# A hybrid attention block on one core: the start of the first projection in halves and product by product, without blank matmuls

## What is computed

```python
u = rms_norm(h, norm_gain)                    # h is x, 512 x 2048
proj = einsum('bsd,de->bse', u, w_in)         # 2048 x 13392
(q_sb, k_sb, v_sb, z_sb, q_sa, k_sa, v_sa, z_sa, q_ix, k_ix, w_ix, g_sb, g_sa) = split(proj)
y_sb = (stick_breaking(q_sb, k_sb, v_sb) * silu(z_sb)) @ w_branch_sb
y_sa = (sparse(q_sa, k_sa, v_sa, q_ix, k_ix, w_ix) * silu(z_sa)) @ w_branch_sa
h = h + (sigmoid(g_sb) * y_sb + sigmoid(g_sa) * y_sa) @ w_out
out = rms_norm(h, final_norm_gain)
```

## Time and profile before

| what | value |
|---|---|
| median of three runs | 1597.24 us (1597.21 to 1597.38) |
| the profiled execution, its own time | 1597.08 us |
| its span, first to last instruction | 1595.5 us |
| PE busy | 1585.0 us, 99% |
| DVE busy | 821.9 us, 52% |
| ACT busy | 572.5 us, 36% |
| DMA read from HBM | 156.9 MB |

### The profile page before, as it was taken

How to read it: one execution, slowest core, us unless ns; L and a number is a source line. 1 busy time by engine, 2 the same in 40 slices (tenths; PEclk the granted TensorE clock), 3 DMA queues, 4 the chain that set the end, 5 groups by cost and what they waited for, 6 DMA issues and landing times.

```text
span 1595.5 us, 19959 instructions
## 1 busy us (share of the span) xinstructions
PE 1585.0 (99%) x7138; PEld 1317.2 (83%) x7138; DVE 821.9 (52%) x1183; ACT 572.5 (36%) x851; POOL 15.8 (1%) x35
## 2 busy tenths in 40 slices
PE   9999999999999999999999999999999999999997
PEld 7788888888888888888888888888888888888886
DVE  6853678522126655556564546554545545434333
ACT  5542333222224444334453332343332533323232
POOL 0000000000000000000000000000000000000000
PEclk9999999999999999999999999999999999999999
DMA  7223323333333333333334334333433522253223
GB/s 225 82 79 93 93 80 93 106 92 85 100 105 96 111 108 110 111 106 104 106 117 132 109 102 113 98 116 110 115 91 122 181 101 92 96 204 121 98 100 118
DMA packets 97979, 176.39 MB, mean 111 GB/s; under 512 B 11264, under 2 KB 24080, under 8 KB 97296
## 3 DMA queue, kind: packets, MB, share of 16 engines
q1 hardware_dynamic: 93712, 160.60, 33.4%
q0 software_dynamic: 3040, 13.63, 2.3%
q10 hardware_dynamic: 1184, 1.58, 0.3%
HBM read 156.90 MB, written 8.39 MB: 104 GB/s over the span
## 4 chain that ended last, share of the span: by engine, by line
PE 97%; ACT 1%; DVE 1%; DMA 1%; issue 0%; SPq 0%; ACTq 0%; DVEq 0%
PE proj L1178 29%; PE proj L1179 29%; PE proj L1180 29%; PE attn L1179 3%; PE attn L1180 3%; PE attn L1178 3%; DMA xs<-in_x 1%; PE attn L1313 1%; PE attn L1312 1%; ACT junk L463 0%; ACT w_hi L410 0%; DVE w_lo L721 0%; DVE xs L764 0%; DVE area L764 0%; ACT u_hi L443 0%
## 5 line engine op out<-in xcount | busy, mean ns | idle before, releaser
L1178 PE MATMUL proj<-u_hi,w_hi 128*128 128x512 f32 x1536 | 600.5, 391 | 0.5 <-DVE u_lo L774 0.5
L1180 PE MATMUL proj<-u_hi,w_lo 128*128 128x512 f32 x1536 | 598.9, 390 | 0.0
L1179 PE MATMUL proj<-u_lo,w_hi 128*128 128x512 f32 x1536 | 598.8, 390 | 0.0
L721 DVE TENSOR_TENSOR w_lo<-stage,w_hi 128x1024 fp32r<-128x1024 f32 x266 | 323.5, 1222 | 458.7 <-ACT w_hi L410 457.2
L410 ACT ACTIVATE w_hi<-stage 128x1024 fp32r<-128x1024 f32 x266 | 280.1, 1056 | 430.9 <-PE proj L1180 302.2
L1178 PEld LDWEIGHTS proj<-u_hi,w_hi 128*128 128x128 f32 x1536 | 288.8, 188 | 60.2 <-issue 1.3
L1180 PEld LDWEIGHTS proj<-u_hi,w_lo 128*128 128x128 f32 x1536 | 288.5, 188 | 60.2
L1179 PEld LDWEIGHTS proj<-u_lo,w_hi 128*128 128x128 f32 x1536 | 288.8, 188 | 58.7
L1178 PE MATMUL proj<-w_hi,u_hi 128*128 128x512 f32 x256 | 99.9, 390 | 0.0
L1180 PE MATMUL proj<-w_hi,u_lo 128*128 128x512 f32 x256 | 99.8, 390 | 0.0
L1179 PE MATMUL proj<-w_lo,u_hi 128*128 128x512 f32 x256 | 99.8, 390 | 0.0
(11 more groups left out here) (175 smaller groups left out, 1413.0 us busy)
## 6 DMA issues: line engine op xcount, KB each, us to landing
stage<-in_w_in SPq DMA_DIRECT2D x208, 512.0 KB, 3.7
stage<-in_w_out SPq DMA_DIRECT2D x32, 512.0 KB, 3.6
x_in<-turned SPq DMA_DIRECT2D x256, 40.0 KB, 1.9
stage<-in_w_branch_sb SPq DMA_DIRECT2D x16, 512.0 KB, 3.6
stage<-in_w_branch_sa SPq DMA_DIRECT2D x16, 512.0 KB, 4.1
xs<-in_x SPq DMA_DIRECT2D x8, 512.0 KB, 8.0
o_scratch<-og POOLq DMA_DIRECT2D x16, 256.0 KB, 2.3
hres<-in_x POOLq DMA_DIRECT2D x1, 4096.0 KB, 13.6
```

The source lines that it names most:

```text
L721: V.tensor_tensor(w_lo[:, s % RING, :, :], stage[:, s % 2, :, :], w_hi[:, s % RING, :, :].bitcast(F), ALU.subtract).then_inc(strip_lo, 1)
L1178: nc.tensor.matmul(out_, a_hi, b_hi, start=start, stop=False, skip_group_check=free)
L1179: nc.tensor.matmul(out_, a_hi, b_lo, start=False, stop=False, skip_group_check=free)
L1180: return nc.tensor.matmul(out_, a_lo, b_hi, start=False, stop=stop, skip_group_check=free)
```

## The change

- SP loads the first slab of x and the first strip of W in halves of 128 channels or rows (256 KB each), in turns: x half 0, W half 0, x half 1, W half 1. The x halves have rows of 512 bytes. Each first half has a semaphore of its own (x_first, first_loaded).
- Strip 2 of W is put ahead of slab 3 of x (it was behind slab 4), and strip 3 ahead of slab 5 (it was behind slab 7).
- DVE, no longer ACT, makes the upper part of the first W half (`tensor_copy`, L789 of the new file), and makes its lower part before u_lo(0); the second W half's lower part comes before u_lo(1).
- PE issues no blank matmuls. The first strip is issued product by product: four matmuls hi times hi, then hi times lo, then lo times hi, each group with its own wait. turn_x(1) stands behind the first group.

```diff
--- before.py
+++ after.py
@@ -121,7 +121,6 @@
     ixw_lo = at("ixw_lo", [KT, KW], R, work + 6 * TILE + 8 * KT * KW)
     junk = at("junk", [D_MODEL], F, place["u_lo"] + 12 * TILE)
     gain_rows = at("gain_rows", [P], F, place["late"])
-    blank = at("blank", [CW], R, place["late"] + 4 * P)
     rstd_row = at("rstd_row", [SEQ], F, place["late"] + 4 * P + 4 * CW)
     rstd_cols = at("rstd_cols", [QT, P], F, work + 14 * TILE)
 
@@ -217,10 +216,11 @@
     gain_loaded, ixw_loaded, consts, masks = sem("gain_loaded"), sem("ixw_loaded"), sem("consts"), sem("masks")
     sumsq, norm_step, rooted = sem("sumsq"), sem("norm_step"), sem("rooted")
     cols_ready, cols_turned, row_ready = sem("cols_ready"), sem("cols_turned"), sem("row_ready")
+    x_first, first_loaded = sem("x_first"), sem("first_loaded")
     first_hi, first_lo = sem("first_hi"), sem("first_lo")
     raw_ready, raw_scaled, un_hi_ready, un_lo_ready = (
         sem("raw_ready"), sem("raw_scaled"), sem("un_hi_ready"), sem("un_lo_ready"))
-    gain_turned, gain_ready, blank_ready = sem("gain_turned"), sem("gain_ready"), sem("blank_ready")
+    gain_turned, gain_ready = sem("gain_turned"), sem("gain_ready")
     xt_done, u_hi_ready, u_lo_ready = sem("xt_done"), sem("u_hi_ready"), sem("u_lo_ready")
     ixw_hi_ready, ixw_lo_ready, kw_done, kw_scaled = sem("ixw_hi_ready"), sem("ixw_lo_ready"), sem("kw_done"), sem("kw_scaled")
     kix_hi_ready, kix_lo_ready = sem("kix_hi_ready"), sem("kix_lo_ready")
@@ -307,16 +307,18 @@
             def first_strip(s):
                 load_strip(C_QIX, s, rows(win)(s)[:, :, COL_QIX:COL_QIX + CW])
 
-            load_x(0)
-            first_strip(0)
+            for k, x_sem, w_sem in ((0, x_first, first_loaded), (1, x_loaded[0], strip_loaded[0])):
+                sp.dma_start(xs[:, :, P * k:P * k + P], x_cols[:, :, P * k:P * k + P]).then_inc(x_sem, 16)
+                sp.dma_start(stage[:, 0, k, :], rows(win)(0)[:, k, COL_QIX:COL_QIX + CW]).then_inc(w_sem, 16)
             load_x(1)
             first_strip(1)
-            for p in range(2, 5):
-                load_x(p)
+            load_x(2)
             first_strip(2)
+            load_x(3)
+            load_x(4)
+            first_strip(3)
             for p in range(5, NS):
                 load_x(p)
-            first_strip(3)
             sp.dma_start(ixw[:, :, :], win[:, :, COL_KIX:COL_KIX + KW]).then_inc(ixw_loaded, 16)
             for s in range(4, NS):
                 first_strip(s)
@@ -470,9 +472,8 @@
             act.wait_ge(gain_ready, 1)
             turned_high(0)
             act.wait_ge(strip_loaded[0], 16)
-            A(w_hi[:, 0, 0, :], stage[:, 0, 0, :], ACT.Copy).then_inc(first_hi, 1)
+            A(w_hi[:, 0, 1, :], stage[:, 0, 1, :], ACT.Copy).then_inc(strip_hi, 1)
             turned_high(1)
-            A(w_hi[:, 0, 1, :], stage[:, 0, 1, :], ACT.Copy).then_inc(strip_hi, 1)
             split_hi(0, 1)
             turned_high(2)
             turned_high(3)
@@ -750,7 +751,6 @@
                 step(V.tensor_tensor(rstd[:, cols], y_, t_, ALU.mult))
 
 
-            V.memset(blank[:, :].bitcast(F), 0.0).then_inc(blank_ready, 1)
             for h in range(HEADS):
                 V.memset(slope[:, h:h + 1], -(2.0 ** (-8.0 * (h + 1) / HEADS)))
             dve.wait_ge(masks, 2)
@@ -785,15 +785,17 @@
                     V.tensor_tensor(by_tile(u_lo[:, k, :]), raw_u(k), by_tile(u_hi[:, k, :].bitcast(F)),
                                     ALU.subtract).then_inc(un_lo_ready, 1)
 
-            dve.wait_ge(gain_ready, 1)
-            turned_low(0)
+            dve.wait_ge(first_loaded, 16)
+            V.tensor_copy(w_hi[:, 0, 0, :], stage[:, 0, 0, :]).then_inc(first_hi, 1)
             dve.wait_ge(first_hi, 1)
             V.tensor_tensor(w_lo[:, 0, 0, :], stage[:, 0, 0, :], w_hi[:, 0, 0, :].bitcast(F),
                             ALU.subtract).then_inc(first_lo, 1)
-            turned_low(1)
+            dve.wait_ge(gain_ready, 1)
+            turned_low(0)
             dve.wait_ge(strip_hi, 1)
             V.tensor_tensor(w_lo[:, 0, 1, :], stage[:, 0, 1, :], w_hi[:, 0, 1, :].bitcast(F),
                             ALU.subtract).then_inc(strip_lo, 1)
+            turned_low(1)
             turned_raw(0)
             turned_raw(1)
             split_lo(0, 1)
@@ -1219,7 +1221,9 @@
                         steps[s]()
 
             def turn_x(k):
-                if k % 2 == 0:
+                if k == 0:
+                    pe.wait_ge(x_first, 16)
+                elif k == 1 or k % 2 == 0:
                     pe.wait_ge(x_loaded[k // 2], 16)
                 if k >= HEAD_START:
                     pe.wait_ge(raw_ready, bank_user(k) + 1)
@@ -1234,35 +1238,32 @@
                 if ts[-1] == KT - 1:
                     m.then_inc(kw_done, 1)
 
-            def keep_busy(n):
-
-                for _ in range(n):
-                    nc.tensor.matmul(proj[3][:, :], blank[:, 0:P], blank[:, :], start=True, stop=True)
-
-            pe.wait_ge(blank_ready, 1)
-            keep_busy(4)
             pe.wait_ge(masks, 1)
             pe.wait_ge(gain_loaded, 16)
             nc.tensor.transpose(kw_bank[:, 0:KT], gain_rows[0:KT, :], ident[0:KT, 0:KT]).then_inc(gain_turned, 1)
-            keep_busy(1)
             turn_x(0)
-            turn_x(1)
-            keep_busy(4)
 
             def first_strip():
 
                 for j in range(2):
-                    pe.wait_ge(u_lo_ready, j + 1)
-                    if j == 0:
-                        pe.wait_ge(first_lo, 1)
-                    else:
+                    def products(w, u, first=False):
+                        for e in range(4):
+                            m = nc.tensor.matmul(proj[e][:, :], w[:, 0, j, P * e:P * e + P], u[:, j, :],
+                                                 start=first, stop=False)
+                        return m
+
+                    if j:
                         turn_x(2)
                         turn_x(3)
-                        pe.wait_ge(strip_lo, 1)
-                    for e in range(4):
-                        cols = slice(P * e, P * e + P)
-                        m = mm3(proj[e][:, :], w_hi[:, 0, j, cols], w_lo[:, 0, j, cols],
-                                u_hi[:, j, :], u_lo[:, j, :], j == 0, False)
+                    pe.wait_ge(u_hi_ready, j + 1)
+                    pe.wait_ge(strip_hi if j else first_hi, 1)
+                    products(w_hi, u_hi, first=j == 0)
+                    if j == 0:
+                        turn_x(1)
+                    pe.wait_ge(u_lo_ready, j + 1)
+                    products(w_hi, u_lo)
+                    pe.wait_ge(strip_lo if j else first_lo, 1)
+                    m = products(w_lo, u_hi)
                 m.then_inc(strip_used, 1)
 
             def between_strips(s):
```

## The result

| | before | with the change |
|---|---|---|
| median of 20 runs each | 1597.52 us (1596.98 to 1598.12) | 1600.18 us (1598.96 to 1601.77) |
| ratio | | 1.0017, 95% interval 1.001 to 1.0023 |
| span of the profiled execution | 1595.5 us | 1597.8 us |

The kernel became 2.7 us slower, with more spread from run to run. The forecast was +1.0 us, with a range up to 1599.6: too small, and the range missed the median.

A forecast was written before the change was run, and what follows sets the result against it. PE, busy 1585.0 of 1595.5 us, bounded the kernel, with the start's end set near 42.2 us by the chain from the first square; slab 3 landing 1.5 + 0.1 us later gave +1.0, so 1598.2 us, range 1596.4 to 1599.6.

The forecast's parts named there:

- The rule for the end: End moves by the larger of the first square's shift from 13.11 and PE's shift at 22.09 less 1.1 us.
- PE's first product: Start of PE's first strip: first real product at 6.2 us instead of 8.35, worth nothing by itself.
- ACT's lead: ACT before the sums: one 0.63 us copy less; squares could start at 12.35 (early clock) or 13.95 (late).
- the two cases: TensorE's rise to 2.4 GHz at 8.6 us (PE 0.75 us early) or about 12.1 (0.85 us late).
- rival 2: TensorE's clock rises late in the first strip: 1599.0, or 1600.2 if low throughout the strip; chance 0.12.
- SP's order: Load queue: strip 2 ahead of slab 3 makes the slab land one transfer, 1.5 us, later; the deciding term.
- The wait costs nothing: SP's wait before strip 2: empty-queue landings 12.1 and 12.6 precede the full queue's 12.5 and 14.0, so no cost.
- the 8.6 that I had allowed: SP's wait: it begins to cost only if the second lower part ends after 12.5 - 3.9 = 8.6 us.
- My 8.2 us for the issue: SP may issue strip 2 at 8.2 us, after the first strip's second lower part, which ended at 9.46 before.
- The 12.6 for slab 3 in an empty queue: Slab 3, issued 0.5 us behind strip 2 and taking 3.9 us in an empty queue, could land at 12.6.
- The price of packets of 512 bytes: Slab 0's halved rows: 0.1 us taken in the sum, bounds 0 to 0.3 us.
- my rivals: Alternatives: PE's lead comes through 0.13, clock rises late 0.12, slower by over 0.2% 0.03, no effect 0.01.

The follow-up runs named there:

- e1: The changed kernel with SP's old load order; halves, product order and missing blanks stay: 1597.84 us, ratio 1.0003.
- e2: The kernel before with only SP's new order (strip 2 ahead of slab 3, strip 3 ahead of slab 5): 1600.57 us, ratio 1.002.
- e4: The changed kernel with slab 0 of x in one transfer, W's first strip still in halves: 1599.80 us, ratio 1.0016.
- e5: The changed kernel with thirteen blank matmuls in PE's long wait, behind the transposes of tiles 6 and 7: 1599.72 us, ratio 1.0014.
- e6: The kernel before with strip 2 right behind slab 2, without a wait, into its own tile in two transfers: 1598.10 us, ratio 1.0003.
- e12: The changed kernel with W's first strip in one transfer, x's first slab still in halves: 1598.89 us, ratio 1.0013.
- e3: The changed kernel with six blank matmuls back at the start, four before the gain, two after four transposes: 1601.47 us, ratio 1.0026.
- e7: The kernel before with the eight sums of squares spread over ACT's idle gaps: 1596.45 us, ratio 0.9994.
- e8: The changed kernel with the sums of squares spread as in e7: 1597.23 us, ratio 0.9999.
- e9: The changed kernel with e3's six blanks and the squares two a strip, all behind strip 2's upper part: 1595.39 us, ratio 0.9988.
- e10: e9 with strip 2 loaded into a tile of its own, without the wait: 1595.01 us, ratio 0.9986.
- e11: e10 with slab 0 of x in one transfer: 1596.24 us, ratio 0.9993.

## Why the prediction was wrong, point by point

**The rule for the end held.** The end moves with the first square as long as PE isn't later. In eight kernels with the squares in their old place the shift of the first square (us) and that of the span were:

| kernel | first square | its shift | shift of the span |
|---|---|---|---|
| changed | 15.43 | +2.3 | +2.3 |
| e1 | 14.05 | +0.9 | +0.9 |
| e2 | 15.48 | +2.4 | +2.3 |
| e4 | 16.15 | +3.0 | +3.0 |
| e5 | 16.46 | +3.4 | +3.3 |
| e6 | 14.13 | +1.0 | +1.0 |
| e12 | 15.37 | +2.3 | +2.2 |
| e3 | 16.28 | +3.2 | +5.2 |

Only e3 leaves the line, by the clock. e7 to e11 then show it from the other side: move the squares, and slab 3's landing stops mattering.

**PE's first product, the copy on DVE, ACT's lead** came as said: 5.73 (said 6.2), a copy of 0.43 us that nothing waited for, strip 1 done 0.5 us early. The clock at the start was neither of the two cases but between them: the first eight products were 0.40 to 0.47 us apart on average, and from 9.93 on 0.23, and the transposes of tiles 2 and 3 started at 10.86, where I had 10.55 and 12.15. So rival 2, whose 1600.2 is next to the measured 1600.18, is not what happened: PE was early at the end of strip 1, and the nearness of the number is chance.

**SP's order** was named as the deciding term, and its first part was sized right: strip 2's place costs 1.0 us on the first square (e6), as the forecast had in all.

"The wait costs nothing" is the step that failed. It rested on a queue that is full the whole time and on a slab's 3.9 us from issue to landing in an empty queue, so that strip 2 could be issued until 8.6 us without loss. The runs show another price. "From issue" is strip 2's time to its landing, "behind slab 2" the time between the two landings, all from the profiled execution, landings to 0.1 us:

| kernel | strip 2 issued | from issue | behind slab 2 | slab 3 landed |
|---|---|---|---|---|
| e6, no wait | 3.64 | | 1.4 | 14.0 |
| e12 | 8.25 | 5.6 | 2.6 | 15.3 |
| e4 | 8.51 | 6.2 | 3.5 | 16.0 |
| e3 | 9.16 | 5.5 | 2.8 | 16.2 |
| changed | 9.16 | 4.7 | 1.9 | 15.4 |
| e2 | 9.73 | 4.2 | 3.3 | 15.3 |
| e5 | 10.17 | 4.7 | 2.0 | 16.4 |

Behind SP's wait strip 2 took 4.2 to 6.2 us, never 3.9, and slab 3 followed it by 1.3 to 1.5 us. Without the wait strip 2 landed 1.4 us behind slab 2. The nearest comparison is e2 with e6 (which also moves the strip in two transfers): the wait cost 1.35 us on the first square, and the times say the same, +2.0 us for e2's four early runs and +0.7 for e6's median. In e2 part of that is a queue that stood empty for a moment (115 GB/s from 10 to 12 us). But e12 issued at 8.25 and e4 at 8.51, both within the 8.6 that I had allowed, and slab 3 landed 1.3 and 2.0 us later than in e6, where 0.1 us or less is from slab 2's own landing. So an empty queue is not the whole of it. In e12 bytes of later transfers went ahead of the strip's last ones; why they did is open.

My 8.2 us for the issue was wrong too. "Its W half is in when all of strip 0 was" failed: the queue did not keep its rate through the four half transfers, 242 GB/s where the earlier trace rows of a full queue had 349. The second W half landed at 7.8 instead of 6.8, slab 2 at 11.9 instead of 11.0, and the issue came at 9.16. By my own bound that lateness would have cost 0.6 us, but no run shows that it cost anything: e12 issued when I had said, and its first square is at 15.37 against 15.43. (The 12.6 for slab 3 in an empty queue also left out the 1.5 us that it takes behind strip 2; with them it is 13.6, still before 14.0.)

The price of packets of 512 bytes, 0.1 us in the sum, is not what failed: the 25 GB/s of e12 over 3 us are 75 KB, or 0.2 us, if they are more than the spread. The Trainium skill's extra cycles for each small packet ("DMA: Bandwidth & Descriptors", section "Why small descriptors are slow (HBM only)") came, in my estimate, to 0.13 us for the slab. The larger part of the dip came with W's halves, whose packets kept their size. Why is not settled; halving alone isn't it, since e6 loads strip 2 in halves behind whole slabs, landing at 12.5, and its queue moved 369 GB/s from 10 to 12 us.

The two losses don't add up. e2 has no halves and its first square is as late as the changed kernel's (15.48 and 15.43), and e1, with halves and the old order, lost 0.9. That the wait hides what the queue lost before would fit; it is not shown.

**The clock, a second time.** The median is 0.4 us beyond the profiled execution's shift, and the spread grew. None of my rivals had the mechanism: I looked for a clock that rises late, not for one that rises and falls again. The later chain and PE's lead made a stretch of 4.3 us with nothing but eight transposes in it (20.84 to 25.19), where the kernel before has 1.6 us with eight (21.30 to 22.87). e3 shows the fall and its price in the rows, and in e5, with that stretch filled, the runs above 1600.5 us are gone. The changed kernel's own profiled execution has no such fall, so that its later runs are this mechanism is concluded and not seen. The mean granted clock of each run supports it: 0.999 in the nine runs up to 1600.01 us, 0.998 or 0.997 in the eleven above. (An estimate from e3: 5 us at half the clock take 0.0016 off the mean.) It is no proof, as three of e5's runs have 0.998 without being later. Nor is PE's lead needed: e2 has none, its stretch is 3.2 us (22.04 to 25.24), and seven of its eleven runs are late, while e12 with 4.1 us has two of ten. How long the stretch is does not order the kernels by itself.

The Trainium skill's rule that I cited against taking the blanks out is that activity releases the clock ("TensorE: Matmul & The Clock Gate", section "Part 1: The HAM clock gate"). e3 and e5 agree with it, but at another place: putting blanks back at the start (e3) made it worse, and where they helped was the wait.

**The range** failed for one reason: it treated slab 3's landing as known to 0.3 us, because the queue was taken as always full. The bound that was missing is a price for SP's wait: 1.35 us in e2, and over 1 us even in e12.

## What to carry to other kernels

Before putting a transfer that waits ahead of one that doesn't, don't take the wait as free because its end plus an empty queue's landing time comes out early enough: here it cost over 1 us even with the issue 3 us ahead of the landing before it (e12), and a tile of its own (e6), which needs no wait, took the cost away. A sum of squares needs all of its input; in a chain it should stand behind the work that needs less, in gaps that the engine has anyway: here that was worth 0.9 us to the old kernel and 2.8 to the changed one, and with blanks at the start and no wait of SP the new start ends 2.2 us ahead of the old kernel. And an engine's lead that ends in a longer wait can cost more than nothing: in e3, where lead and late slab came together, the clock fell in it.

## What was not expected of the hardware

- TensorE's granted clock fell from 1.00 to 0.50 in a wait of 3.4 and 1.3 us with four transposes between, and stayed there for 5 us of dense products (e3).
- A strip of 512 KB that SP issued behind a wait landed 4.2 to 6.2 us after its issue, and the landing did not follow the issue: issued at 8.51 (e4) it landed at 14.7, issued at 9.16 (changed) at 13.8.
- With four transfers of 256 KB at its head the queue moved 242 to 268 GB/s from 4 to 7 us, and 329 to 362 with whole ones of 512 KB.
- In executions with the same early transfers the landing of slab 3 moved by 1 us (15.4 in the changed kernel, 16.4 in e5, 16.2 in e3 with strip 2 issued at the same 9.16).
